# A two-block transformer stack in one kernel: its first loads cut into halves, its first norm moved forward, its last norm reordered

## What is computed

```python
def rms_norm(x, g):
    y = x * lax.rsqrt(jnp.mean(x * x, axis=-1, keepdims=True) + 1e-6)
    return y * g

def swiglu_ffn(h, w_gate, w_up, w_down):          # 1024 -> 2816 -> 1024
    return (jax.nn.silu(h @ w_gate) * (h @ w_up)) @ w_down

# block A, for each of 2 layers: FFN, mixer (stick-breaking attention, conv, GLA), FFN
x = x + 0.5 * rms_norm(swiglu_ffn(rms_norm(x, pre), w_gate, w_up, w_down), post)
...
# block B, for each of 2 layers: mixer (RG-LRU, forgetting attention, retention), cross attention, FFN
x = x + rms_norm(swiglu_ffn(rms_norm(x, pre), w_gate, w_up, w_down), post)
```

## Time and profile before

| | |
|---|---|
| time, median of 3 runs | 2033.84 us (2033.42 to 2034.59) |
| the profiled execution's own time | 2034.0 us |
| its span in the trace | 2032.2 us |
| PE busy in the span | 2012.7 us (99%) |
| DVE busy | 1434.9 us (71%) |
| ACT busy | 1122.7 us (55%) |
| HBM read | 365.66 MB, 180 GB/s over the span |
| chain of work that ended last, by engine | PE 91%, DVE 5%, ACT 2%, DMA 1%, issue 1% |

### The profile page before, as it was taken

One profiled execution on the slowest core, in us unless ns is written; L12 is line 12 of the kernel. 1 busy time (PEld: TensorE's weight loads), 2 busy tenths in 40 slices (PEclk: granted clock), 3 DMA queues, 4 the chain that ended last, 5 costly groups with the idle time before them and its releaser, 6 DMA issues.

```text
span 2032.2 us, 24477 instructions
## 1 busy us (share of the span) xinstructions
PE 2012.7 (99%) x9706; PEld 1663.8 (82%) x9706; DVE 1434.9 (71%) x1901; ACT 1122.7 (55%) x1413; POOL 0.2 (0%) x4
## 2 busy tenths in 40 slices
PE   7999999999999999999999999999999999999998
PEld 6888887888888888887888888898888887988887
DVE  6656899776667566899776567966765669567565
ACT  6445657664446455666564446756644457565443
POOL 0000000000000000000000000000000000000000
PEclk9999999999999999999999999999999999999999
DMA  8766764567776875764557767544677675446674
GB/s 276 215 204 183 223 201 145 173 195 203 214 215 211 235 212 171 225 195 145 184 184 215 211 185 214 186 146 137 191 215 203 189 206 186 162 139 187 207 214 123
DMA packets 342931, 392.47 MB, mean 193 GB/s; under 512 B 115344, under 2 KB 251168, under 8 KB 342816
## 3 DMA queue, kind: packets, MB, share of 16 engines
q1 hardware_dynamic: 338720, 379.85, 62.1%
q10 hardware_dynamic: 4096, 11.05, 1.5%
HBM read 365.66 MB, written 1.05 MB: 180 GB/s over the span
## 4 chain that ended last, share of the span: by engine, by line
PE 91%; DVE 5%; ACT 2%; DMA 1%; issue 1%; SPq 0%; ACTq 0%; DVEq 0%
PE ps L612 81%; PE ps L1110 2%; DVE w_lo L1860 1%; PE ps L683 1%; DVE scratch L2138 1%; PE ps L1212 1%; PE ps L1193 1%; DVE x L1910 0%; DMA raw<-in_ffn_w_up 0%; ACT w_hi L1272 0%; DVE scratch L2175 0%; PE ps L758 0%; DMA x<-in_x 0%; PE ps L1058 0%; PE ps L706 0%
## 5 line engine op out<-in xcount | busy, mean ns | idle before, releaser
L1860 DVE TENSOR_TENSOR w_lo<-raw,w_hi 128x2048 fp32r<-128x2048 f32 x337 | 770.1, 2289 | 230.1 <-ACT w_hi L1272 227.4
L1272 ACT ACTIVATE w_hi<-raw 128x2048 fp32r<-128x2048 f32 x341 | 646.0, 1898 | 466.1 <-PE ps L612 212.7
L612 PE MATMUL ps<-w_hi,hT_hi 128*128 128x512 f32 x2048 | 806.0, 394 | 0.7 <-DVE w_lo L1860 0.7
L612 PE MATMUL ps<-w_lo,hT_hi 128*128 128x512 f32 x2048 | 798.0, 390 | 0.0
L612 PE MATMUL ps<-w_hi,hT_lo 128*128 128x512 f32 x2048 | 774.1, 389 | 0.0
L612 PEld LDWEIGHTS ps<-w_hi,hT_hi 128*128 128x128 f32 x2048 | 384.9, 188 | 84.3 <-issue 5.5
L612 PEld LDWEIGHTS ps<-w_hi,hT_lo 128*128 128x128 f32 x2048 | 384.4, 188 | 80.5
L612 PEld LDWEIGHTS ps<-w_lo,hT_hi 128*128 128x128 f32 x2048 | 385.0, 188 | 77.0
L612 PE MATMUL ps<-w_hi,bT_hi 128*128 128x512 f32 x592 | 232.1, 392 | 1.4 <-DVE bT_lo L1951 1.4
L612 PE MATMUL ps<-w_hi,bT_lo 128*128 128x512 f32 x592 | 230.5, 389 | 0.0
L612 PE MATMUL ps<-w_lo,bT_hi 128*128 128x512 f32 x592 | 230.5, 389 | 0.0
(11 more groups left out here) (299 smaller groups left out, 1293.4 us busy)
## 6 DMA issues: line engine op xcount, KB each, us to landing
raw<-in_w_in SPq DMA_DIRECT2D x160, 512.0 KB, 4.7
raw<-in_ffn_w_down SPq DMA_DIRECT2D x88, 512.0 KB, 4.3
raw<-in_ffn_w_gate SPq DMA_DIRECT2D x87, 512.0 KB, 4.0
raw<-in_ffn_w_up SPq DMA_DIRECT2D x87, 512.0 KB, 5.0
raw<-in_w_gate SPq DMA_DIRECT2D x44, 512.0 KB, 4.0
raw<-in_w_up SPq DMA_DIRECT2D x44, 512.0 KB, 5.0
raw<-in_w_down SPq DMA_DIRECT2D x44, 512.0 KB, 4.4
raw<-in_w_out SPq DMA_DIRECT2D x32, 512.0 KB, 4.5
```

The lines of the kernel that those rows point to most:

```text
L612: mm = nc.tensor.matmul(bank(t, half), act[:, tiles[i], t * P:(t + 1) * P], w, start=start and (i, n) == steps[0], stop=stop and (i, n) == ...
L1272: nc.scalar.activation(dst, src, ACT.Copy).then_inc(high_ready, 1)
L1860: V.tensor_tensor(lo, src, flat(hi), ALU.subtract).then_inc(low_ready, 1)
```

## The change

Five edits.

1. `x` is loaded as four DMAs of 256 KB, by column half and then row tile, each with a semaphore of its own. The 16 transposes, ACT's copies and DVE's low parts of the first norm follow that order: (t0, half 0), (t1, half 0), (t0, half 1), (t1, half 1).
2. Unit 1 is loaded, rounded and subtracted in two pieces like unit 0. SP issues it when row tile 1's first half of `x` has landed, where it waited for all of row tile 0.
3. ACT's two squares of the first norm stand between `high` of unit 1 and unit 3, and its two roots directly behind unit 3, ahead of the last loads of constants.
4. ACT takes a root of a constant column before its first copy, so that the first table loaded holds the root.
5. In the very last norm DVE runs `bias(1)` and `weigh(1, 0)` ahead of `add(0, 1)`.

```diff
+    def turned_at(L, j, t, kh):
+        return 2 * t + kh if L.sub0 + j else 2 * kh + t
...
-            if u == 0:
+            if u < 2:
+                if u:
+                    sp.wait_ge(x_loaded[TT - 1][0], 16)
                 for i in range(2):
                     for dst, src in halves:
-                        sp.dma_start(dst[:, 2 * i:2 * i + 2, :], src[:, 2 * i:2 * i + 2, :]).then_inc(first_landed[i], 16)
+                        sp.dma_start(dst[:, 2 * i:2 * i + 2, :], src[:, 2 * i:2 * i + 2, :]).then_inc(
+                            first_landed[u][i], 16)
                 return
-            if u == 1:
-                sp.wait_ge(x_loaded[0], 16)
...
-        for t in range(TT):
-            for kh in range(2):
+        for kh in range(2):
+            for t in range(TT):
                 norm_turn(Layer("A", 0), 0, t, kh)
...
-            norm_in(L, j)
+            if L.sub0 + j:
+                norm_in(L, j)
...
-        act.dma_start(x[:, 0, :], d["x"][0, 0:P, :]).then_inc(x_loaded[0], 16)
-        act.dma_start(x[:, 1, :], d["x"][0, P:T, :]).then_inc(x_loaded[1], 16)
+        for h in range(2):
+            for t in range(TT):
+                act.dma_start(x[:, t, 512 * h:512 * h + 512],
+                              d["x"][0, t * P:(t + 1) * P, 512 * h:512 * h + 512]).then_inc(x_loaded[t][h], 16)
...
-        first_unit_high(0)
+        act.wait_ge(*after("start", "warm", 0))
+        nc.scalar.activation(root_warm, root_warm, ACT.Sqrt).then_inc(*done("start_root", "table"))
+        first_units_high(0, 0)
         act.wait_ge(gains_ready, 1)
...
+        first = Layer("A", 0)
+        turned(first, 0, 0, 0)
+        first_units_high(0, 1)
+        turned(first, 0, 1, 0)
+        turned(first, 0, 0, 1)
+        first_units_high(1, 0)
+        turned(first, 0, 1, 1)
+        first_units_high(1, 1)
+        square_in(first, 0, 0)
+        high(first, 2)
+        square_in(first, 0, 1)
+        high(first, 3)
+        root_in(first, 0)
...
-            add(0, 1)
-            bias(1)
-            weigh(1, 0)
             if outputs_end(L, j + 1):
+                bias(1)
+                weigh(1, 0)
+                add(0, 1)
                 weigh(1, 1)
                 scale(1)
                 add(1, 0)
                 add(1, 1)
                 return
+            add(0, 1)
+            bias(1)
+            weigh(1, 0)
```

More of the change, by code:

```diff
@@ L329, in _program @@
     gains_loaded, post_loaded, pack_loaded = sem("gains_loaded"), sem("post_gain_loaded"), sem("pack_loaded")
-    ident_loaded, x_loaded = sem("ident_loaded"), [sem(f"x_loaded{t}") for t in range(TT)]
+    ident_loaded, x_loaded = sem("ident_loaded"), [[sem(f"x_loaded{t}{h}") for h in range(2)] for t in range(TT)]
     x_ready, sq_in, std_ready, rstd_ready = sem("x_ready"), sem("sq_in"), sem("std_ready"), sem("rstd_ready")
@@ L334, in _program @@
     gains_turned, gains_ready = sem("gains_turned"), sem("gains_ready")
-    first_landed, first_high, first_low = [sem(f"first_landed{i}") for i in range(2)], sem("first_high"), sem("first_low")
+    first_landed = [[sem(f"first_landed{u}{i}") for i in range(2)] for u in range(2)]
+    first_high, first_low = sem("first_high"), sem("first_low")
     sq_out, sq_bias, std_out_ready, rstd_out_ready = sem("sq_out"), sem("sq_bias"), sem("std_out"), sem("rstd_out")
@@ L382, in x_is_ready @@
         else:
-            engine.wait_ge(x_loaded[t], 16)
+            for i in range(h + 1):
+                engine.wait_ge(x_loaded[t][i], 16)
     def ffn_outputs(L, n, k):
@@ L653, in wait @@
                         bank_free(t)
-                    if L.sub0 + j == 0 and (n, t, i) == (0, 0, 2):
-                        weights(L, k)
-                    pe.wait_ge(hT_hi_ready, L.sub(j, 16, 8 * t + firsts[n] + i + 1))
+                    if L.sub0 + j == 0 and (t, i) == (0, 2):
+                        weights(L, k + n)
+                    pe.wait_ge(hT_hi_ready, L.sub(j, 16, 4 * turned_at(L, j, t, firsts[n] // 4) + i + 1))
                 return wait
@@ L1285, in rows_of, with square_in, root_in @@
             return out_b if L.b else out_a
-        def norm_in(L, j):
-            for t in range(TT):
-                x_is_ready(act, L, j, t, 1)
-                nc.scalar.activation(rows_of(L)[:, t, :], x[:, t, :], ACT.Square,
-                                     accum_out=ss_in[:, t:t + 1]).then_inc(sq_in, 1)
+        def square_in(L, j, t):
+            x_is_ready(act, L, j, t, 1)
+            nc.scalar.activation(rows_of(L)[:, t, :], x[:, t, :], ACT.Square,
+                                 accum_out=ss_in[:, t:t + 1]).then_inc(sq_in, 1)
+        def root_in(L, j):
             gain(post_g, L.sub0 + j, 1, post_loaded)
@@ L2670, in _ @@
         enter(Layer("A", 0))
+        V.memset(root_warm, 1.0).then_inc(*done("start", "warm"))
         V.memset(uT[:, :, 0:CPAD], 0.0).then_inc(*done("start", "pad"))
@@ L2675, in _ @@
         dve.wait_ge(gains_ready, 1)
-        first_unit_low(0)
-        for t in range(TT):
-            for kh in range(2):
-                if (t, kh) == (1, 1):
-                    weight_low(Layer("A", 0), 1)
-                low(Layer("A", 0), 0, t, kh)
-                if (t, kh) == (0, 0):
-                    first_unit_low(1)
+        first = Layer("A", 0)
+        first_units_low(0, 0)
+        low(first, 0, 0, 0)
+        first_units_low(0, 1)
+        low(first, 0, 1, 0)
+        low(first, 0, 0, 1)
+        first_units_low(1, 0)
+        low(first, 0, 1, 1)
+        first_units_low(1, 1)
         for k in range(2, AHEAD + 1):
-            weight_low(Layer("A", 0), k)
+            weight_low(first, k)
         for l in range(DEPTH):
```

41 lines of the change are left out of this document (18 added, 23 removed).

## The result

| | before | after |
|---|---|---|
| median | 2033.79 us (22 executions, fastest 2032.66) | 2036.93 us (22 executions, 2034.15 to 2038.75) |
| ratio | | 1.0015, 95% interval 1.0009 to 1.0021 |
| the profiled execution's own time, span | 2034.0, 2032.2 us | 2036.24, 2034.5 us |

The changed kernel is 3.1 us slower. That is within 0.2%, but above the range of the forecast (2031.7 to 2035.1), and the interval excludes a ratio of 1. The profiled execution shows 2.3 of the 3.1 us in its span.

The account below looks back on a forecast made before the run. PE bounds the kernel, busy 2012.7 of 2032.2 us, so only gains still there at 37.35 us count. Gains of 0.3 us there and 0.1 at the end sum to 0.4, giving a 2033.4 us median, range 2031.7 to 2035.1.

Parts of the forecast that it names:

- the landing of the quarters: Start: x's first quarter lands at 7.8 us, second 8.7 to 9.3, last 10.3; first matmul 0.8 us earlier, at 11.3.
- the release that hung on the second of them: Start: SP issues unit 1 at 8.7 to 9.3 us instead of 8.75, once x's second quarter has landed.
- The rule's estimate: Start: by queues taking turns per packet, row tile 1's first half lands some 0.3 us later than 512 KB did before.
- I let unit 6 land at 33.6 again: Ahead of unit 4: same bytes through full DMA engines, so unit 6 lands unchanged and its rounding ends at 35.54 us.
- rival B: Start: unit 1's release is d later (at most 1.5 us), all weights too; at d = 1.0, 2034.4 us; chance 16%.
- The forecast's own sign of being wrong: Unit 6's rounding starts over 0.5 us away from 33.6, or PE arrives at unit 4 later than 35.9 us.
- what is late next: Unit 4: PE arrives at 34.6 us, waits about 2.4 for unit 6's rounding, starts at 37.05; 0.3 us gain kept.
- rival C: Unit 4: the longer wait lets PE's clock fall, 2.6 us lost, giving 2036.0 us; chance 7%.
- the end: Last norm on DVE: reordering removes one 0.10 us gap; gain 0.1 us, bounds 0 and 0.2.
- Slower would need C and B together: Whole kernel: a loss beyond 0.2% (4.1 us) needs rival C and rival B at once; chance of slower 3%.
- the saved table load: ACT: one table load of 1.28 us has gone, so silu starts near 25.7 us instead of 27.93.
- rival A: Unit 4: unit 6 does not hold PE, the start's gain passes through; gain 1.4 + 0.1, 2032.3 us; chance 22%.

Follow-up runs that it names:

- e4_tail: The kernel before with only the last norm reordered (bias(1) and weigh(1, 0) ahead of add(0, 1)); 2033.10 us, ratio 0.9997.
- e2_gate: The changed kernel, but SP issues unit 1 when row tile 0's first half of x has landed; 2035.62 us, ratio 1.0009.
- e16_endfill: The kernel before plus four idle PE matmuls behind all of PE's work; 2033.75 us, ratio 1.0002.
- e9_stall_half: The kernel before plus one 128x512 subtraction on DVE ahead of unit 4's low part, delaying PE; 2035.72 us, ratio 1.0009.
- a_again: The changed kernel run and profiled once more, unedited; 2037.39 us, ratio 1.0018.
- e3_wholex: The changed kernel with x again in two whole row tiles, SP released by the first, former column order; 2035.07 us, ratio 1.0006.
- e5_stall: The kernel before plus one 128x1024 subtraction on DVE ahead of unit 4's low part, delaying PE; 2036.35 us, ratio 1.0012.
- e7_before_const: The kernel before with the late constants issued behind unit 6's rounding; 2037.99 us, ratio 1.0022.
- e8_undo1_const: The changed kernel with x in whole row tiles again and the late constants issued behind unit 6's rounding; 2033.26 us, ratio 0.9996.
- e11_undo1_const_fill: The changed kernel with whole x tiles, late constants behind unit 6's rounding and four idle PE matmuls ahead of unit 4; 2033.74 us, ratio 0.9998.
- e10_null: The kernel before plus four idle PE matmuls inside its wait for unit 4; 2034.57 us, ratio 1.0002.

## Why the prediction was wrong

The median fell outside the range because three steps failed together: the landing of the quarters, the release that hung on the second of them (0.8 us), and the clock (1.6 us).

**Failed: "I put its landing 0.9 us ahead of 8.7, at 7.8; the first halves of both tiles are again half the bytes, 8.7 to 9.3; the last quarter lands at 10.3 as before".** The first quarter landed near 8.9, the second near 9.9 and the last at 11.4. (By the forecast's own rate, 256 KB at 0.23 MB/us, the lead would have been 1.1 us, not 0.9; nothing hangs on it.) The queues from 5 to 8 us (packets, MB, share), against the earlier trace rows:

```profile
q10 hardware_dynamic: 257, 0.48, 51.8%
q1 hardware_dynamic: 266, 0.26, 28.9%
```

Before, ACT's queue got 187 packets of some 4 KB to SP's 216; now it gets 257 of 2 KB to 266. In both cases the two queues have about the same number of packets, so ACT's queue moves 0.48 MB in place of 0.70. I had taken its rate in bytes from the earlier trace rows as a constant, and it went with the packet's size: 0.48 to 0.53 MB in all six profiles with halves, 0.66 to 0.75 in nine of the ten with whole tiles (0.94 in e4_tail). A quarter of `x` and a whole tile are both 128 rows. The Trainium skill has a rule for it (DMA: Bandwidth & Descriptors, "Queues, rings and completion order": an engine takes turns between the queues, a packet at a time). The counts of packets agree with it; I had the rule in the prediction and gave the row the preference. The rule's estimate for row tile 1's first half, 0.3 us later than the whole tile had been, was nearer than mine, but it measured 1.2 (9.9 against 8.7). An estimate from the count of packets comes closer: at 257 in 3 us the second quarter's 128 rows take 1.5 us behind the first's, and it landed 1.0 behind. Over all profiles the first transpose starts at 8.46 to 9.04 us in the six with halves (mean 8.77) and at 8.50 to 9.03 in nine of the ten with whole tiles (7.55 in e4_tail; median 8.62). Half the bytes landed no earlier. With that fell the first matmul at 11.3 (12.48) and unit 1's start at 18.0 (19.08), so that PE reached unit 4 at 35.56, not 34.6.

**Failed: unit 1's release, "SP issues at 8.7 to 9.3", and with it "I let unit 6 land at 33.6 again".** SP issued unit 1 at 9.94, rival B's d = 1.2 us, and unit 6 was rounded from 34.81. In every profile with that release, the issue came 1.0 us behind the first transpose, which is the distance of the two quarters. Rival B had the right place, the right range (up to 1.5) and the right sum: PE's start at unit 4 would be 37.05 + 1.2 = 38.25, measured 38.14, and e2_gate took back the 0.8 us. Its chance (16%) hung on the landing above. The forecast's own sign of being wrong was there: unit 6's rounding 1.2 us from 33.6.

**Incomplete: "what is late next".** The forecast followed unit 6 alone. Unit 5 is as late, and through its subtraction on DVE it holds the join to within 0.1 us of the same time. So do the transposes, put at "near 34.5" and landed at 35.8. It changed no number here, but with unit 6 alone early the join would still have held PE. It was missed also that DVE's reciprocal (26.47) queues behind a unit's subtraction (24.26 to 26.55), so silu came at 26.72 and not at 25.7. Unit 0's first piece was delayed by 2.1 us on ACT (rounded from 7.44 instead of 5.37), not by 1.3; the cover of more than 2 us held.

**Failed: "with the granted clock at 1.00", rival C at 7%.** The mechanism and the sign were right, the chance was not: the only pause known to be harmless was 1.43 us, and the forecast itself lengthened it to 2.4. All profiles together, sorted by PE's wait at unit 4:

| clock stayed at full | clock fell |
|---|---|
| under 0.2, 0.8, 1.1, 1.2, 1.2, 1.3 us, and 1.4 in before, e16_endfill and e4_tail | 2.0 (e2_gate), 2.0 (e9_stall_half), 2.6 (after), 2.8, 2.9, 4.1, 4.7 us |

In six of these seven the clock was low for 3.4 us, in a_again for 6.8. The price, the offset at 57 us less that at 53, was 1.4 to 1.6 us for the shorter stretch (after 1.59, e2_gate 1.62, e3_wholex 1.40, e5_stall 1.55, e7_before_const 1.61, e9_stall_half 1.61) and 2.2 for the longer, not the 2.6 that I took from the start's 5.1 us. The Trainium skill's section (TensorE: Matmul & The Clock Gate, "HAM oscillation — how this bites in real kernels") describes the effect for waits of 3 to 5 us; here 2.0 us had it, and the measurement decides.

**Failed: the two rivals taken as separate.** They feed each other. A release that is late by d lengthens the wait by d, and the longer wait takes the clock. With d = 1.2, a price of 1.6 and 0.2 us from the end, the forecast's own sum gives 37.05 + 1.2 - 37.35 + 1.6 - 0.2 = 2.3 us of loss, which is the difference of the two spans to 0.1 us. "Slower would need C and B together" was in the text, at 3%, but for a loss beyond 0.2%; B and C had chances of their own, 16 and 7%, and the range left C out.

**Right.** The gone wait for unit 1's low part; unit 1's second piece in time; the longer wait at unit 4 and why the start's gain ends in it (e3_wholex: start earlier, PE at unit 4 no earlier); the saved table load without any further drain; the end, 0.2 us within its bounds of 0 and 0.2.

**Open.** The median lost 3.1 us, the profile explains 2.3. a_again shows what makes up the rest in some executions (later units and a longer low clock). The mean clocks say that it fell in at least 14 of the 22 (and in the profiled one), not how long PE waited in each. What decides whether the clock falls at a wait near 2 us, as it did in some executions of e9_stall_half and not in others, is open. And why the landing of one weight unit near 1800 us moves by a microsecond when four matmuls are added 1760 us earlier is not known. No kernel tried the first quarter of `x` at 7.8 us, so rival A (the gain passes through) was tested only through the constants: with PE's start 1.6 us earlier and the clock up (e8_undo1_const, e11_undo1_const_fill), 1.7 us of gain lasted to 1793 us in e11's profile (an execution 0.8 us below its median), and in e8 it was spent by 57 us in the second wait. e4_tail's profile, where `x` and the weights behind it happened to come 1.2 us early, kept it all.

## What to carry to other kernels

A wait that grows costs more than its length once it lets PE's clock fall; in this kernel's profiles waits up to 1.4 us cost only themselves, and those of 2.0 us and more cost 1.4 to 2.2 us on top, so a gain ahead of a fixed landing can be worse than none. Cutting a DMA into halves that shorten its rows cut what it got beside another queue in 3 us from 0.70 to 0.48 MB here, and a release hung on the second of the halves delays all that is queued behind it. When a landing is what bounds, ask of the neighbours too (here unit 5 beside unit 6): several landings move together, and they move from execution to execution.

## What the runs showed that was not expected

- Two queues at work at once had about equal numbers of packets, whatever the size: 187 to 216 with 4 KB rows beside 1 KB rows, 257 to 266 with 2 KB rows; in e4_tail, where `x` landed earliest, 246 to 244. All the bytes moved from 5 to 8 us fell with it, from 0.91 to 0.74 MB.
- The granted clock fell at pauses of 2.0 us (e2_gate, e9_stall_half) and stayed at 1.4 us, and the low stretch began anywhere from 2.2 us ahead of PE's restart (a_again, 37.30 and 39.51) to 0.7 us behind it (e7_before_const, 39.99 and 39.25).
- 0.5 us of delay added at one place cost 2.1 us by 57 us (e9_stall_half's profile), and 2.3 us of median.
- Four matmuls that fill an existing wait, and cost nothing there, were followed by a gap of PE near 1802 us (1.0 to 1.2 us from one matmul's start to the next) in each of the four kernels that had them, where the others had none; in e10_null behind a unit that landed 1.3 us later.
